# A two-part transformer stack in one Trainium2 kernel: two of the grouped layer's four query blocks, with their norms and turns, emitted between its attention units, and five smaller edits of order

## The reference, cut to what matters

```python
def gqa_axial_mixer(h, hc, w_in, q_norm, k_norm, w_out, ctx_out):
    def project(t):
        q, k, v = split(t @ w_in, [8*128, (8+2)*128])   # 8 query heads, 2 key heads, 2 value heads
        q = rmsnorm(q per head, q_norm); k = rmsnorm(k per head, k_norm)
        return q, k, v
    q, k, v = project(h);  qc, kc, vc = project(hc)
    q, k = apply_rope_2(q, cos, sin), apply_rope_2(k, cos, sin)
    k_all, v_all = concat([kc, k]), concat([vc, v])     # 512 keys
    return softmax(q @ k_all.T * 128**-0.5) @ v_all @ w_out
```

## Time and profile before

| quantity | value |
|---|---|
| median of 3 runs | 2727.27 us (2722.51 to 2729.57) |
| the profiled execution | 2721.09 us |
| its span, first to last instruction | 2719.4 us |
| TensorE matmuls busy | 2522.3 us, 93% |
| TensorE weight loads (beside the matmuls) | 2397.8 us, 88% |
| VectorE busy | 1694.0 us, 62% |
| ScalarE busy | 1241.3 us, 46% |
| moved by DMA | 480.12 MB, mean 177 GB/s |

### The profile page before, as it was taken

How to read it: one execution, slowest core, us unless ns; L and a number is a source line. 1 busy time by engine, 2 the same in 40 slices (tenths; PEclk the granted TensorE clock), 3 DMA queues, 4 the chain that set the end, 5 groups by cost and what they waited for, 6 DMA issues and landing times.

```text
span 2719.4 us, 48514 instructions
## 1 busy us (share of the span) xinstructions
PE 2522.3 (93%) x20604; PEld 2397.8 (88%) x20604; DVE 1694.0 (62%) x2846; ACT 1241.3 (46%) x1674; POOL 1.2 (0%) x6
## 2 busy tenths in 40 slices
PE   6789998999999999999988998999999999887998
PEld 5679997888989999999887898999999999766998
DVE  5565565556766556566767576577655557746655
ACT  4443343444445444445445453455444345434443
POOL 0000000000000000000000000000000000000000
PEclk9989999999999999999898999999999999888999
DMA  6546656533556665544351354554444555363453
GB/s 234 217 171 242 246 195 236 211 109 125 189 194 232 233 224 185 174 162 148 126 173 63 110 182 144 185 182 175 171 163 179 185 175 183 120 213 141 170 179 117
DMA packets 71590, 480.12 MB, mean 177 GB/s; under 512 B 8784, under 2 KB 9296, under 8 KB 17744
## 3 DMA queue, kind: packets, MB, share of 16 engines
q1 hardware_dynamic: 66240, 468.74, 48.2%
q10 hardware_dynamic: 5136, 8.28, 1.0%
HBM read 471.48 MB, written 1.05 MB: 174 GB/s over the span
## 4 chain that ended last, share of the span: by engine, by line
PE 74%; DVE 12%; ACT 6%; DMA 4%; issue 3%; ACTq 0%; DVEq 0%
PE bank L263 66%; ACT whi L222 3%; DMA raw<-w_main 2%; DVE wlo L242 2%; PE bank L1102 2%; DVE wlo L229 2%; DMA raw<-w_down 1%; PE bank L984 1%; DVE tmpx L626 1%; DVE HX L632 1%; PE bank L922 1%; DVE ARX L675 1%; PE bank L549 1%; PE bank L972 1%; PE bank L1624 0%
## 5 line engine op out<-in xcount | busy, mean ns | idle before, releaser
L263 PE MATMUL bank<-HNX_hi,whi 128*128 128x256 f32 x2968 | 862.4, 291 | 64.5 <-DVE wlo L242 24.2
L222 ACT ACTIVATE whi<-raw 128x2048 fp32r<-128x2048 f32 (+1 forms) x378 | 706.0, 1868 | 369.4 <-PE bank L263 183.1
L263 PE MATMUL bank<-HNX_hi,wlo 128*128 128x256 f32 x2968 | 846.4, 286 | 0.0
L263 PE MATMUL bank<-HNX_lo,whi 128*128 128x256 f32 x2968 | 831.7, 285 | 0.0
L229 DVE TENSOR_TENSOR wlo<-raw,whi 128x1024 fp32r<-128x1024 f32 (+1 forms) x378 | 453.3, 1199 | 585.9 <-ACT whi L222 585.4
L263 PEld LDWEIGHTS bank<-HNX_hi,whi 128*128 128x128 f32 x2968 | 578.3, 195 | 90.5 <-issue 49.4
L263 PEld LDWEIGHTS bank<-HNX_hi,wlo 128*128 128x128 f32 x2968 | 579.2, 195 | 0.0
L263 PEld LDWEIGHTS bank<-HNX_lo,whi 128*128 128x128 f32 x2968 | 570.2, 195 | 1.1 <-issue 0.9
L242 DVE TENSOR_TENSOR wlo<-raw,whi 128x1024 fp32r<-128x1024 f32 (+1 forms) x378 | 450.7, 1192 | 0.0
L263 PE MATMUL bank<-HNC_hi,whi 128*128 128x256 f32 x1344 | 389.7, 290 | 13.7 <-DVE HNC_lo L689 4.3
L263 PE MATMUL bank<-HNC_lo,whi 128*128 128x256 f32 x1344 | 381.7, 284 | 0.0
(11 more groups left out here) (342 smaller groups left out, 2920.0 us busy)
## 6 DMA issues: line engine op xcount, KB each, us to landing
raw<-w_main SPq DMA_DIRECT2D x270, 1024.0 KB, 4.8
raw<-w_ada SPq DMA_DIRECT2D x72, 1024.0 KB, 4.8
raw<-w_down SPq DMA_DIRECT2D x72, 1024.0 KB, 4.9
raw<-w_down SPq DMA_DIRECT2D x36, 768.0 KB, 4.2
raw<-w_cmp SPq DMA_DIRECT2D x4, 1024.0 KB, 4.7
tmpx<-ARX ACTq DMA_DIRECT2D x18, 128.0 KB, 5.3
tmpx<-ARX ACTq DMA_DIRECT2D x32, 64.0 KB, 4.6
HX<-x_in SPq DMA_DIRECT2D x2, 512.0 KB, 6.1
```

Source lines behind the costliest of these rows:

```text
L222: NS.activation(WHI[q % HIS][:, 0:size], RAW[m % SLOTS][:, 0:size], ACT.Copy).then_inc(sems["w_hi"], 1)
L263: return NT.matmul(dst, (WHI[ordinal[n] % HIS], WLO[n % SLOTS])[w][:, k * 2 * P + col:k * 2 * P + col + P], x[xp][:, kx, :], start=start, ...
```

## The change

Six edits:

- `early` is now always false: at the start of the program, too, the a lane takes one modulation block beside every second dense block.
- `Between.run` is a generator, so that a job may hold a dense block with its yields.
- In the grouped layer, query blocks 2 and 3 stay ahead of the attention; blocks 4 and 5 are emitted ahead of its steps 1 and 5. The steps, exchanges and turns of queries 2, 3 and 4 move to steps 1 to 10, and the second turn's exchange goes behind `want("kv1")`. Sums and spreads of the heads use bank 4, and scores banks 2 and 3 in place of 0 and 1.
- `table_of(func)` is a new activation of one column whose result nobody reads. It is put where ScalarE's function is about to change: before the square roots of a norm, after the last root in front of a feed-forward stage (`then=ACT.Tanh`), and before the attention (`ACT.Exp`).
- `spread_out` makes both diagonals by one product of 128x256.
- In the x lane's norms with a residual, `scale(0)` is emitted ahead of the root and `add_back(0)` behind the diagonals.

```diff
@@ class Between @@
     def run(self, step):
         for job in self.later.pop(step, ()):
-            job()
+            blocks = job()
+            if blocks is not None:
+                yield from blocks
@@ norm and its helpers @@
+            def table_of(func):
+                if act:
+                    NS.activation(SMALL[:, 126:127], vec("eps6"), func)
...
                 if on(dve, inv, *ready):
-                    for j in range(2):
-                        op = NV.tensor_scalar(buf[:, j * P:(j + 1) * P], ident, SMALL[:, at + j:at + j + 1], None, MUL)
-                    op.then_inc(diag.sem, 1)
+                    NV.tensor_tensor(buf.rearrange("p (c q) -> p c q", c=2), ident.unsqueeze(1).to_broadcast([P, 2, P]),
+                                     SMALL[:, at:at + 2].unsqueeze(2).to_broadcast([P, 2, P]), MUL).then_inc(diag.sem, 1)
...
                 if post:
+                    if t == "x":
+                        table_of(ACT.Sqrt)
...
+                ahead_of_root = post and t == "x"
+                first = scale(0) if ahead_of_root else None
                 inv = inverse_root(S, known, small(S, HH), S.col + RMS_H)
+                if then is not None:
+                    table_of(then)
                 diag = spread_out(S.col + RMS_H, S.SQ[-1], S.wide_h, inv, now(f"{t}_sq_sum"), now(f"{t}_total"))
+                if ahead_of_root:
+                    add_back(0, first)
...
-                    nxt = scale(j) if post and j < KD else None
-                    if post and 1 <= j <= KD:
+                    nxt = scale(j) if post and ahead_of_root <= j < KD else None
+                    if post and ahead_of_root < j <= KD:
                         add_back(j - 1, sc)
@@ attend @@
-                    between.run(it)
+                    yield from between.run(it)
@@ pace @@
-                    early = (0, 1) not in gains_known
+                    early = False
@@ norms ahead of feed-forward stages; before each attention @@
-                x = yield from norm(X, True, pre(X, 1, 2), y[-1:], mods)
+                x = yield from norm(X, True, pre(X, 1, 2), y[-1:], mods, then=ACT.Tanh)
...
+                table_of(ACT.Exp)
@@ grouped layer @@
-(BANK[3], 0), (BANK[2], 0), shared) for i, t in enumerate(tiles)]
+(BANK[4], 0), (BANK[4], 0), shared) for i, t in enumerate(tiles)]
...
-                for b in range(5):
-                    if b >= 4:
-                        rotate(b - 4)
-                    if b >= 3:
-                        send(b - 3)
-                    if b >= 2:
-                        steps[b - 2][2]()
-                    if b >= 1:
-                        steps[b - 1][1]()
-                    steps[b][0](z[-1] if b else z[0])
-                    if b < 4:
-                        z = yield from linear(X, "ga_in", [(2 + b, 4 + 2 * b)], Z)
+
+                def queries(b, *jobs):
+                    z = yield from linear(X, "ga_in", [(b, 2 * b)], Z)
+                    for job in jobs:
+                        job()
+                    steps[b - 1][0](z[-1])
+                steps[0][0](z[0])
+                yield from queries(2, steps[0][1])
+                yield from queries(3, steps[0][2], lambda: send(0), steps[1][1])
                 want("kv1")
                 passed.add("ga")
-                yield ("L", 2.0)
-                steps[3][2]()
-                steps[4][1]()
+                yield ("L", 1.0)
+                steps[1][2]()
+                send(1)
+                steps[2][1]()
+                rotate(0)
+                yield ("L", 1.0)
                 rotate(1)
-                send(2)
...
-                between.at(1, lambda: (steps[4][2](), rotate(2), send(3)))
-                between.at(2, lambda: send(4))
-                between.at(3, lambda: rotate(3))
-                between.at(4, lambda: rotate(4))
+                between.at(1, steps[2][2])
+                between.at(1, lambda: send(2))
+                between.at(1, lambda: queries(4))
+                between.at(3, lambda: rotate(2))
+                between.at(3, steps[3][1])
+                between.at(4, steps[3][2])
+                between.at(4, lambda: send(3))
+                between.at(5, lambda: queries(5))
+                between.at(6, lambda: rotate(3))
+                between.at(7, steps[4][1])
+                between.at(8, steps[4][2])
+                between.at(8, lambda: send(4))
+                between.at(10, lambda: rotate(4))
...
-                                      lambda u, a: (BANK[u % 2], 0), BANK[6], BANK[7], between, lambda u: [roped[1 + u // 4]])
+                                      lambda u, a: (BANK[2 + u % 2], 0), BANK[6], BANK[7], between, lambda u: [roped[1 + u // 4]])
```

More of the change, by code:

```diff
@@ L581, in square_sum, with norm @@
                 return kept
-            def norm(S, post, pre, ready, mod=(), opening=False):
+            def norm(S, post, pre, ready, mod=(), opening=False, then=None):
                 t, known = S.tag, ready[-1]
@@ L775, in tile_norm @@
                         NS.activation(b.rearrange("p (a q) -> p a q", a=2), src, ACT.Square).then_inc(sq.sem, 1)
+                    if j == 0 and not S.lag:
+                        table_of(ACT.Sqrt)
                     yield ("L", 0.8)
@@ L1340, in x_sequence @@
                 y = yield from linear(X, "ev_out", OUT, None, ready=mixed, gain=gain1("mix_post", 0))
-                x = yield from norm(X, True, (gain1("ffn_pre", 0), None), y[-1:])
+                x = yield from norm(X, True, (gain1("ffn_pre", 0), None), y[-1:], then=ACT.Tanh)
                 yield from ffn(X, 0, gain1("ffn_post", 0), x)
@@ L1661, in x_sequence @@
                 y = yield from linear(X, "od_out", OUT, None, ready=mixed, gain=gain1("mix_post", 1))
-                x = yield from norm(X, True, (gain1("ffn_pre", 1), None), y[-1:])
+                x = yield from norm(X, True, (gain1("ffn_pre", 1), None), y[-1:], then=ACT.Tanh)
                 urge[0] = 1
@@ L1665, in x_sequence @@
                 mods = need(0, 0, 1)
-                x = yield from norm(X, True, pre(X, 0, 0), [now("x_evac")], mods)
+                x = yield from norm(X, True, pre(X, 0, 0), [now("x_evac")], mods, then=ACT.Tanh)
                 urge[0] = 2
@@ L1727, in x_sequence @@
                 mods = need(0, 6, 7)
-                x = yield from norm(X, True, pre(X, 0, 2), y[-1:], mods)
+                x = yield from norm(X, True, pre(X, 0, 2), y[-1:], mods, then=ACT.Tanh)
                 free["x", "gain"] = need(0, 8)
@@ L1731, in x_sequence @@
                 mods = need(1, 0, 1)
-                x = yield from norm(X, True, pre(X, 1, 0), [now("x_evac")], mods)
+                x = yield from norm(X, True, pre(X, 1, 0), [now("x_evac")], mods, then=ACT.Tanh)
                 free["x", "gain"] = need(1, 2)
@@ L1795, in x_sequence @@
                 o = yield from attend(X, units, float(np.float32(P ** -0.5)), PB, PT, None, [vt, roped[0], *kv_ready["kv1"]],
-                                      lambda u, a: (BANK[u % 2], 0), BANK[6], BANK[7], between, lambda u: [roped[1 + u // 4]])
+                                      lambda u, a: (BANK[2 + u % 2], 0), BANK[6], BANK[7], between, lambda u: [roped[1 + u // 4]])
                 while between.later:
-                    between.run(min(between.later))
+                    yield from between.run(min(between.later))
                 mixed = [mixed[h] for h in range(8)]
```

## The result

The changed kernel takes 2733.97 us (median of 20 runs, 2726.89 to 2742.05), the kernel before 2727.29 us on the same chips (20 runs). The ratio is 1.0028, 95% interval 1.0021 to 1.0035: 7.6 us slower, where 6.9 us faster was forecast. The time lies within the range given, the sign is wrong. The miss of 14.5 us has two parts of like size, the opening and the grouped layer; the norms and tables came out as forecast.

What follows compares the result with a forecast made beforehand. TensorE was busy 2522.3 of 2719.4 us, so only its 197 us standing and low-clock stretches could be won. Opening -9.4, norms -3.5, tables +0.5, grouped layer +5.5 made -6.9: 2720.4 us, range 2709 to 2736.

Steps and rivals of the forecast that it cites:

- Opening, -9.4: Program start: `ev_out` 9.1 us earlier, two modulation blocks fewer 2.1, context norm moved 2.5, less 4.3; bounds -14 and 0.
- the four modulation blocks come back later ... 4.3 in all: Opening: the four return among dense blocks where nothing hides them, 16 matmuls and 1.07 us each.
- Norms and tables, -3.0: x lane norms -3.5 us from fewer operations and one diagonal product; early table loads +0.5 us.
- Grouped layer, +5.5: Moving two query blocks into the attention was to cost 5.5 us net, new waits outweighing filled holes.
- Small holes filled: Grouped layer's attention, 94% full: moved query blocks fill 1.8 of its 2.5 us of idle time.
- context +1.0: Grouped layer: context must be finished 15 us sooner, lengthening the wait before its block by 1.0 us; bounds 0 and +3.
- Exchange +3.7: Grouped layer: second turn's exchange, now issued behind the context's blocks, is waited for 3.7 us; bounds +1 and +6.4.
- Third unit +6.2: Attention: last moved query block's split waits on ACT for its late load, 6.2 us; bounds 0 and +8.
- `ga_out` -4.9: Grouped layer: the 6.41 us stall before `ga_out` shrinks to about 1.5, winning 4.9 us; bounds -6.4 and 0.
- Tables +1.3: Attention: four more table loads among exponentials, 5.1 us on ACT, charged at 1.3 us; bounds 0 and 5.1.
- The opening gives nothing: Rival, chance 0.10: vector chain and gating's tail end where they did; +2.5 us in all, 2729.8.
- ACT is held in the attention: Rival, chance 0.15: three holes of 6.41 us, grouped layer costs 25.3 us; whole +12.9, 2740.

Runs made afterwards that it cites:

- e1: Kernel before with `early = False` alone; 2725.36 us, ratio 0.9994 to the kernel before.
- e4: Changed kernel with the grouped layer's order of before; 2722.59 us, ratio 0.9980 to the kernel before.
- e3: Kernel before with the edits in and around the norms and the table loads alone; 2723.60 us, ratio 0.9989.
- e2: Kernel before with the grouped layer's new order, `Between` and banks alone; 2738.95 us, ratio 1.0044.
- e9: Changed kernel with sums of keys and queries 2, 3 in bank 3, spreads of keys and queries 2 in bank 2; 2734.37 us, ratio 1.0028.
- e6: Changed kernel with query block 5 emitted ahead of attention step 2 in place of step 5; 2732.90 us, ratio 1.0019.
- e7: Changed kernel with a scaled copy for the root of queries 4 and 5 (four heads wrong); 2737.99 us, ratio 1.0031.

## Why the prediction was wrong

- *Opening, -9.4.* Its working held to the end of `ev_out`: reciprocal, splits and start of `ev_out` within 0.5 us, and the lead at 400 us (13.6 in e1, 11.9 after, 10.2 in e4 against e3) is the forecast's 9.1 + 2.1 + 2.5 = 13.7 or somewhat less. The step that failed is "the four modulation blocks come back later ... 4.3 in all". They cost some 5.1 ("late" has 3.8 for three of them, the fourth is taken at the same price), with a new hole of 1.55 us beside them. And, unforeseen, their absence ahead of the odd layer puts TensorE's instruction loads at a bad place there: +7 on average (78.3 us in before, e2 and e3 against 85.1 in e1, e4 and after), 4.7 of it idle time. In all -12 + 5.1 + 1.6 + 7 = +1.7, where -1.6 [-4.1, +1.1] was measured; some 3 us stay open, as much as the clock alone moves one trace.
- *Norms and tables, -3.0.* Right: -3.0 [-5.5, -0.5]. That a load taken from the gate brings nothing is borne out by the 1.47 us there. How the sum divides (-3.5 for the norms, +0.5 for the tables) no run shows: e3 has both.
- *Grouped layer, +5.5.* Sign right, size off; measured +12.0. The term that failed most is "Small holes filled": -1.8 was forecast, +1.6 found. Idle time grew by 9.9 us. Term by term: context +1.0, found +2.0 (4.25 to 1.93 + 4.30: the bank change, which I had written off as nothing, makes the first of them, though `e9` shows that the wait is there without it too). Exchange +3.7, found +2.9, by another cause (VectorE's order). Third unit +6.2, found 6.41, and for the cause forecast: the changed kernel's chain has the block's load there, issued at 2409.65 and landed 6.54 us later, then its split, and then VectorE's turn and diagonal; `e6` takes the hole away. `ga_out` -4.9, found -3.2. Tables +1.3, found 0.7 at most. Small holes filled -1.8: of 2.5 us none was filled, 0.72, 1.04, 0.92 and a new 1.47 stand where 0.70, 1.11 and 0.71 stood. Without the tables these terms make 9.7 of the 9.9. The rest, some 2 us of the 12.0, I put down to the clock: in the windows below the granted clock is 0.84 through the query blocks that stay and the holes behind them, where TensorE had been full at 1.00, and 0.88 in the attention's first 49 us, against 0.94. (The traces differ by 3.4 us of busy time, but 1.1 of that is the sixteenth modulation block.) I had reckoned stalls at the stalls' own length.

```profile
2409.65 6.54 DMA raw<-w_main
```
```profile
2344.00:2370.00 26.00, 19.21 (x138) 18.39 (x139) 15.92 (x32) 10.72 (x17) 0.00 (x0) 0.84 0.40 135
2401.00:2450.00 49.00, 39.94 (x313) 30.45 (x312) 18.89 (x43) 20.08 (x37) 0.00 (x0) 0.88 0.53 185
```

- *The rivals.* "The opening gives nothing" (0.10) came nearest in size, 2729.8 for 2734, but by another way: its tail did end earlier. "ACT is held in the attention" had one of its three holes. No case had an opening that wins 12 us and loses them in the odd layer and behind it.
- *The Trainium skill* ("ScalarE: Activation LUTs", "What ACT_TABLE_LOAD costs") gives about 2.66 us for a switch of set; four switches more would be 10.6 us of ScalarE. `e7` takes these four away and nothing clear of noise is won, so here their price is hidden by either figure; the row of 1.28 us and the next activation 10 ns behind it stand.

## What to carry to other kernels

Work taken out of a stalling stretch is not gone: price where it lands, with the holes it makes there (here 5.1 + 1.6 for an expected 4.3). Moving full work into a stretch that is 94% busy can win at most its idle 2.5 us, and stalls added can cost more than their length where the clock falls behind them (9.9 us of them, 12.0 in all). In a program whose instructions are fetched while it runs, dropping 136 instructions or adding 128 shifted every later load of them by half a load; compare kernels by the same stretch in many traces, and try a shift before blaming the edit.

## What the runs showed of the hardware

- TensorE's instructions came in 164 loads of 16 KB. Shifting them by half a load with instructions that do nothing lengthened one stretch of the same program from 75.9 to 83.5 us and shortened it from 85.9 to 79.6 and from 85.8 to 80.1, idle time by 3.7, 4.1 and 4.5 us.
- A 1 MB weight transfer took 5.65 to 6.00 us where such a load fell beside it (twelve traces) and 4.70 to 4.94 where none did (eight).
- Exponential and tanh took turns from 521 to 671 us behind one table load; 45 loads of the changed kernel took 1283 ns each.
- 256 waits on a long reached semaphore (128 instructions) held TensorE's first matmul from 11.7 to 20.5 us.
- Up to 2340 us e2 is the program of before, yet its profiled execution reached that point 8.1 us later with 6.9 us less idle time: the granted clock was at its lower level for longer (mean 0.97 against 0.98). One profile of each kernel can't weigh a change of this size; the ratios can.
